# A two-block transformer kernel: latents' factors moved earlier, memory keys and values as products of rounded parts, the heads' norm taken apart, short turns placed inside projections

## The reference, cut to what matters

```python
# first block, per layer: norm, one wide projection, four mixers, output projection
h = _rmsnorm(x, norm_g[l]); p = _split(h @ w_in[l])
o_a = _mla(p["a_cq"], p["a_ckv"], ...)   # latents: _rmsnorm(cq, qa_g) @ w_uq, _rmsnorm(ckv, kva_g) @ w_ukv
o_b = _diff_attn(...); o_c = _dsa(...)   # _dsa: index scores, top-k of 128 keys for each query
o_d = _short_conv(...)
x = x + concat(o * silu(gate)) @ w_out[l]
# second block
x = x + 0.5 * swiglu(rms_norm(x, g_ffn1), ...)
proj = rms_norm(x, g_mix) @ w_in          # q, k, v of 16 heads of 64
oa = dilated_attention(first 12 heads); ob = moba_attention(last 4 heads)
ya = rms_norm(merge_heads(oa), g_out_a)   # over 768 channels
yb = rms_norm(merge_heads(ob), g_out_b)   # over 256 channels
x = x + concat(ya, yb) @ w_out
# cross attention to a memory of 256 tokens
mn = rms_norm(mem, g_mem); k, v = split(mn @ w_ckv)
x = x + attend(rms_norm(x, g_cross) @ w_cq, k, v) @ w_co
x = x + 0.5 * swiglu(rms_norm(x, g_ffn2), ...); return rms_norm(x, g_final)
```

## Time and profile before

| | |
|---|---|
| median of three runs | 1896.84 us |
| the profiled execution | 1894.07 us |
| its span, first to last instruction | 1892.3 us |
| mean granted clock of TensorE | 0.994 |
| DVE busy | 55% |
| ACT busy | 37% |
| POOL busy | 20% |
| mixing stage, steps 0 to 31 | about 1077 to 1323 us of the span |

### The profile page before, as it was taken

How to read it: one execution, slowest core, us unless ns; L and a number is a source line. 1 busy time by engine, 2 the same in 40 slices (tenths; PEclk the granted TensorE clock), 3 DMA queues, 4 the chain that set the end, 5 groups by cost and what they waited for, 6 DMA issues and landing times.

```text
span 1892.3 us, 26241 instructions
## 1 busy us (share of the span) xinstructions
PE 1850.2 (98%) x9284; PEld 1466.0 (77%) x9284; DVE 1037.5 (55%) x2106; ACT 691.6 (37%) x1274; POOL 385.6 (20%) x223
## 2 busy tenths in 40 slices
PE   7999999999999999999999999999999999999998
PEld 4767777876777788888888777777887888888887
DVE  4689787568978756554533333333544654554332
ACT  3444444444444442332232343343323432332222
POOL 2336252433534340000000222230110100000000
PEclk9999999999999999999999999999999999999999
DMA  5212212222221242323333412222221222322332
GB/s 189 68 68 79 65 48 80 91 68 68 78 67 47 78 135 94 100 92 97 100 101 110 150 46 78 78 78 79 90 89 45 68 90 98 100 94 95 103 109 89
DMA packets 48577, 165.65 MB, mean 88 GB/s; under 512 B 5592, under 2 KB 6104, under 8 KB 48472
## 3 DMA queue, kind: packets, MB, share of 16 engines
q1 hardware_dynamic: 47176, 161.88, 26.4%
q10 hardware_dynamic: 1296, 2.42, 0.4%
HBM read 162.12 MB, written 2.17 MB: 87 GB/s over the span
## 4 chain that ended last, share of the span: by engine, by line
PE 92%; DVE 3%; issue 2%; ACT 1%; POOL 1%; DMA 1%; POOLq 0%; DVEq 0%; SPq 0%; ACTq 0%
PE proj L862 73%; PE score L1078 3%; PE o L1114 2%; PE turned L1090 2%; PE proj L1233 2%; PE proj L1237 1%; PE turned L1301 1%; PE score L1295 1%; PE o L1325 1%; PE turned L832 1%; DVE wlo L1791 1%; PE o L1389 1%; PE score L1378 1%; ACT whi L1437 1%; PE proj L992 1%
## 5 line engine op out<-in xcount | busy, mean ns | idle before, releaser
L862 PE MATMUL proj<-hhi,whi 128*128 128x512 f32 x1488 | 598.9, 403 | 6.7 <-POOL wlo L655 2.6
L862 PE MATMUL proj<-hhi,wlo 128*128 128x512 f32 x1488 | 582.1, 391 | 0.0
L862 PE MATMUL proj<-hlo,whi 128*128 128x512 f32 x1488 | 581.9, 391 | 0.0
L1437 ACT ACTIVATE whi<-ring 128x1024 fp32r<-128x1024 f32 x266 | 281.4, 1058 | 679.7 <-PE proj L862 633.7
L862 PEld LDWEIGHTS proj<-hhi,whi 128*128 128x128 f32 x1488 | 280.5, 189 | 101.0 <-issue 33.9
L862 PEld LDWEIGHTS proj<-hhi,wlo 128*128 128x128 f32 x1488 | 280.5, 189 | 60.1
L862 PEld LDWEIGHTS proj<-hlo,whi 128*128 128x128 f32 x1488 | 280.9, 189 | 56.0 <-issue 1.0
L1791 DVE TENSOR_TENSOR wlo<-ring,whi 128x1024 fp32r<-128x1024 f32 x187 | 228.5, 1222 | 158.8 <-ACT whi L1437 158.7
L655 POOL TENSOR_TENSOR wlo<-ring,whi 128x1024 fp32r<-128x1024 f32 x79 | 189.8, 2404 | 445.4 <-ACT whi L1437 445.2
L668 POOL TENSOR_TENSOR prob<-prob 128x512 f32<-128x512 f32 x30 | 46.3, 1543 | 853.6 <-ACT prob L1433 853.2
L1463 ACT ACTIVATE prob<-prob,negmax 128x256 f32<-128x256 f32 (+3 forms) x208 | 114.4, 551 | 160.1 <-DVE negmax L1835 160.1
(11 more groups left out here) (219 smaller groups left out, 2211.0 us busy)
## 6 DMA issues: line engine op xcount, KB each, us to landing
ring<-wstream SPq DMA_DIRECT2D x288, 512.0 KB, 3.4
arena<-lines SPq DMA_DIRECT2D x28, 256.0 KB, 5.5
arena<-x ACTq DMA_DIRECT2D x4, 512.0 KB, 6.4
out<-arena SPq DMA_DIRECT2D x8, 256.0 KB, 2.9
arena<-mem SPq DMA_DIRECT2D x1, 1024.0 KB, 8.8
par<-params ACTq DMA_DIRECT2D x3, 74.0 KB, 1.9
arena<-hot SPq DMA_DIRECT2D x2, 85.0 KB
arena<-rope SPq DMA_DIRECT2D x1, 128.0 KB, 6.4
```

What stands on the lines that cost most here:

```text
L862: mm = pe.matmul(b, rounded(w), rounded(rhs(v, k)), start=(first and n == 0 and p == 0), stop=(last and n == len(blocks) - 1 and p == 2))
L1437: act.activation(rounded(dst), src, ACT.Copy, scale=scale).then_inc(ready, 1)
```

## The change

1. Latents. The sums of squares of CQ0, CQ1 and CKV move from chunks 1, 3, 5 of BK0 to chunks 5 and 7 of BQ0 and chunk 1 of BK0. DVE takes the means after the first half of the top-k, and makes the diagonals after the third and before it takes BK0's result; the spread stands behind the first chunk of VT0. Five top-k halves stand before the steps, the rest inside. On POOL and ACT the slot prepared after KR comes before the key's rotation.
2. Memory keys and values. KV slots are split in high and low parts like all others, the normed memory too (`memhi`, `memlo`). A key job is 8 x 3 rounded products of 128x256. Value slots are loaded so that one holds half of the contraction for two blocks of output channels; two slots make one job with a bank of 512 columns, 24 products of 128x256 each. KV12, KV13 are fills of the last window, KV14 fills steps 32 and 33.
3. Heads' norm. The pairs run in the order 6, 7, 0, ..., 5, so the group of 256 channels comes first. The six chunks of the group of 768 are scaled by gain alone and rounded as each pair ends; MIXOUT's result is multiplied by that group's factor (`residual_heads`). The two others are scaled by the ratio of the factors.
4. Turns (VN, MT), MSUM (in four parts) and MROOT are guests inside projection jobs. A guest that is a job takes the number before its host's.

```diff
+MIX_WINDOWS = (("Q1", "K1", "VT1"), ("Q2", "K2", "VT2"), ("Q3", "K3", "VT3", "KV0", "KV1"), ("Q4", "K4", "VT4", "KV2", "KV3"),
...
+    ("KV8", "KV9", "KV10", "KV11", "KV12", "KV13"))
+MIX_REST, MIX_LAST = "KV14", "KV15"
+PAIR_ORDER = (6, 7, 0, 1, 2, 3, 4, 5)
+GROUP_B = 2
+MIX_GUESTS = {"Q1": {2: "VN0", 4: "MT0"}, "K1": {4: "MT1"}, "VT1": {4: "MT2"}, "Q2": {1: "VN1", 4: "MT3"},
+              "K2": {0: "MSUM", 2: "MSUM", 4: "MSUM", 6: "MSUM"}, "Q3": {1: "VN2", 4: "MROOT"}, "Q4": {1: "VN3"},
+              "Q5": {1: "VN4"}, "Q6": {1: "VN5"}, "Q7": {1: "VN6"}, "KV8": {1: "VN7"}}
...
-LATENT_AT = ((3, 1), (3, 3), (3, 5))
+LATENT_AT = ((2, 5), (2, 7), (3, 1))
-TOPK_FIRST, TOPK_EARLY = 3, 7
+TOPK_FIRST, TOPK_EARLY = 3, 5
...
+            def load_v(n):
+                u, block = (stream_of(n) - PAIR_AT - 4 * KC) % 2, stream_of(n) // 2 * 2
+                src = bass.AP(wstream.tensor, block * P * SLOT + u * 4 * P, [[SLOT, P], [P * SLOT, 2], [1, 4 * P]])
+                sp.dma_start(ring[:, n % RING, :].rearrange("p (b n) -> p b n", b=2), src).then_inc(wload[n % RING], 16)
...
                 prepare_after("KI")
-                after_low(SLOT_OF["CQ0"])
+                prepare_after("KR")
+                after_low(SLOT_OF["CQ1"])
                 pool.wait_ge(krope_moved, L + 1)
...
-                for name in IDX_JOBS:
+                for name in IDX_JOBS[:3]:
                     prepare_after(name)
                 pool.wait_ge(mean_ready, L * 2 + 2)
                 root(2 * NT)
+                prepare_after(IDX_JOBS[3])
...
-                in_job("VT0")
-                pe.wait_ge(spread_ready, L * LAYER_ROOTS + (R_LATENT + 1))
-                spread_roots(turned[1], spread[0][:, 0:NT, :])
-                spread_roots(turned[0], spread[0][:, NT:2 * NT, :]).then_inc(spread_done, 1)
+                for k in range(KC):
+                    in_chunk("VT0", k)
+                    if k == 0:
+                        pe.wait_ge(spread_ready, L * LAYER_ROOTS + (R_LATENT + 1))
+                        spread_roots(turned[1], spread[0][:, 0:NT, :])
+                        spread_roots(turned[0], spread[0][:, NT:2 * NT, :]).then_inc(spread_done, 1)
...
+                    for p, (w, v) in enumerate(((whi[:, h, cols], memhi), (whi[:, h, cols], memlo), (wlo[:, s, cols], memhi))):
+                        mm = pe.matmul(b[:, 0:MEM], rounded(w), rounded(v[:, k, :]), start=(k == 0 and p == 0),
+                                       stop=(k == KC - 1 and p == 2))
...
+                    for p, (w, v) in enumerate(((whi[:, h, :], memhi), (wlo[:, s, :], memhi), (whi[:, h, :], memlo))):
+                        wv = w.rearrange("p (b k n) -> p b k n", b=2, k=4)[:, :, k % 4, :]
+                        mm = pe.matmul(b[:, t * MEM:(t + 1) * MEM].rearrange("p (b n) -> p b n", b=2), rounded(v[:, kk, tok]),
+                                       rounded(wv), start=(u == 0 and k == 0 and p == 0), stop=False, skip_group_check=True)
...
+            for k in range(5):
+                kv_chunk(MIX_LAST, k)
+            for n in range(GROUP_B):
+                add_squares(turned[0], NT, o2sqB[:, n, :], n == 0)
+            pe.wait_ge(o2sq_added, KC - GROUP_B - 2)
+            add_squares(turned[0], 0, o2sq[:, 0, :])
             pe.wait_ge(o2sq_ready, KC)
+            add_squares(turned[0], 0, sq[:, 0, :]).then_inc(o2sum_done, 1)
+            for k in range(5, KC):
+                kv_chunk(MIX_LAST, k)
+            made = KC - GROUP_B
+            mixout_chunks(0, range(made - 1), True)
             pe.wait_ge(spread_ready, R_HEADS + 1)
             spread_roots(turned[1], spread[0][:, 0:NT, :])
             spread_roots(turned[0], spread[0][:, NT:2 * NT, :]).then_inc(spread_done, 1)
+            mixout_chunks(1, range(made - 1))
+            mixout_chunks(0, range(made - 1, made), True)
+            mixout_chunks(1, range(made - 1, made))
+            mixout_chunks(0, range(made, KC), True)
+            mixout_chunks(1, range(made, KC))
+            for c in range(2, KC):
+                mixout_chunks(c, range(KC))
...
# ACT
+                prepare_after("KR")
                 wait_out(act, L, "KR")
                 act.activation(krope[HD:HD + 32, 1, :], krope[HD + 32:P, 1, :], ACT.Copy).then_inc(krope_moved, 1)
-                prepare_after("KR")
...
+            def heads_out(p):
+                square_heads(p)
+                if p >= GROUP_B:
+                    c = PAIR_ORDER[p]
+                    high_y2(c, gain[:, G_OUT + c:G_OUT + c + 1])
...
# DVE
-                        for n in range(TOPK_FIRST):
+                        topk_half(0)
+                        dve.wait_ge(latsum_done, L + 1)
+                        mean_squares(turned[0], ((0, 0, NT, 256), (NT, NT, NT, 128))).then_inc(mean_ready, 1)
+                        for n in range(1, TOPK_FIRST):
                             topk_half(n)
+                        spread_diag(L * LAYER_ROOTS + R_LATENT, spread[0], range(2 * NT)).then_inc(spread_ready, 1)
                     out_of(name, *early[name])
...
+            mean_squares(turned[0], ((0, 0, NT, 768), (NT, NT, NT, 256))).then_inc(heads_step, 1)
+            dve.reciprocal(ms[:, 2 * NT:3 * NT], ms[:, 0:NT]).then_inc(heads_step, 1)
+            dve.tensor_tensor(ms[:, NT:2 * NT], ms[:, NT:2 * NT], ms[:, 2 * NT:3 * NT], ALU.mult).then_inc(mean_ready, 1)
...
+            def residual_heads(c):
+                j = MIX_JOB[f"OUT{c}"]
+                dve.wait_ge(job_done, j + 1)
+                dve.tensor_tensor(tmp[:, c % 2, :], proj[j % 2][:, :], R[:, :], ALU.mult).then_inc(out_step, 1)
+                dve.wait_ge(out_step, c + 1)
+                dve.tensor_tensor(xT[:, c, :], xT[:, c, :], tmp[:, c % 2, :], ALU.add).then_inc(job_free[j % 2], 1)
```

More of the change, by code:

```diff
@@ L107 @@
 MIX_WINDOWS = (
[L108 to L119, removed]
+    ("Q1", "K1", "VT1"),
+    ("Q2", "K2", "VT2"),
+    ("Q3", "K3", "VT3", "KV0", "KV1"),
+    ("Q4", "K4", "VT4", "KV2", "KV3"),
+    ("Q5", "K5", "VT5", "KV4", "KV5"),
+    ("Q6", "K6", "VT6", "KV6"),
+    ("Q7", "K7", "VT7", "KV7"),
+    ("KV8", "KV9", "KV10", "KV11", "KV12", "KV13"))
[5 more added lines that the diff above has]
+              "Q5": {1: "VN4"}, "Q6": {1: "VN5"}, "Q7": {1: "VN6"}, "KV8": {1: "VN7"}}
+MIX_ORDER = ["Q0", "K0", "VT0"] + [part for names in MIX_WINDOWS for name in names
+                                   for part in (*dict.fromkeys(MIX_GUESTS.get(name, {}).values()), name)] \
+    + [MIX_REST, MIX_LAST] + [f"{w}{c}" for w in ("OUT", "CQ", "CO") for c in range(KC)]
+V_FIRST = [f"KV{n}" for n in range(KC, 2 * KC, 2)]
+MIX_JOBS = [name for name in MIX_ORDER if name[:2] != "VN" and name not in V_FIRST]
 MIX_JOB = {name: FFN1_JOB + FFN_JOBS + n for n, name in enumerate(MIX_JOBS)}
+for _n in range(KC, 2 * KC, 2):
+    MIX_JOB[f"KV{_n}"] = MIX_JOB[f"KV{_n + 1}"]
 MIX_TAKE = [name for name in MIX_ORDER if name[:2] not in ("VN", "MT", "MS", "MR")]
@@ L149, in is_split @@
         return n % LAYER_SLOTS not in RAW
-    return not (PAIR_AT <= n < FFN2_AT and MIX_TAKE[n - PAIR_AT][:2] == "KV")
+    return True
 def on_pool(n):
@@ L181, in half_before @@
     return SPLITS[split_no(n) - 2]
-MIX_PREP = {MIX_TAKE[half_before(n) - PAIR_AT]: n for n in range(MIX_SLOT["VT0"], FFN2_AT) if is_pair(n)}
+MIX_PREP = {MIX_TAKE[half_before(n) - PAIR_AT]: n for n in range(MIX_SLOT["VT0"], FFN2_AT) if is_pair(n) or is_kv(n)}
 FFN2_JOB = FFN1_JOB + FFN_JOBS + len(MIX_JOBS)
@@ L277 @@
 MIX_STEPS = 4 * KC
+MIX_FILLED = MIX_STEPS + 2
 def mix_plan():
-    plan = [[] for _ in range(MIX_STEPS)]
+    plan = [[] for _ in range(MIX_FILLED)]
     for w, names in enumerate(MIX_WINDOWS):
@@ L298, in mix_plan @@
             spent += cost
+    for k in range(KC):
+        plan[MIX_STEPS + k // 4].append((MIX_REST, k))
     return plan
@@ L777, in mix_low @@
                     make_low(n % RING, half_of(n), split_no(n) + 1)
-            for name in MIX_ORDER[:4]:
+            for name in MIX_ORDER[:3]:
                 mix_low(name)
[L781 to L786, removed]
+            for s in range(MIX_FILLED):
+                if s - 2 in O2_STEP and O2_STEP[s - 2] > GROUP_B:
+                    p = O2_STEP[s - 2]
+                    pool.wait_ge(o2sq_ready, p + 1)
+                    if p > GROUP_B + 1:
+                        pool.wait_ge(o2sq_added, p - GROUP_B - 1)
                     pool.tensor_tensor(o2sq[:, 0, :], o2sq[:, 0, :], o2sq[:, 1, :], ALU.add).then_inc(o2sq_added, 1)
@@ L1698, in after_mix @@
                 elif what == "KV":
-                    kv_copy(int(name[2:]))
+                    if name not in V_FIRST:
+                        kv_copy(int(name[2:]))
+                    if name in MIX_PREP:
+                        make_high2(MIX_PREP[name])
+                elif what == "MROOT":
+                    for c in range(KC):
+                        if c < KC - 1:
+                            act.wait_ge(memN_ready, c + 1)
+                        else:
```

(5 more changed lines are left out.)

198 lines of the change are left out of this document (106 added, 92 removed).

## The result

The changed kernel takes 1874.95 us (median of 4 runs, 1873.3 to 1876.5) against 1896.25 beside it (1894.1 to 1897.1): ratio 0.9889, 95% interval 0.9872 to 0.9906, so 21 us or 1.1% faster. The forecast was 1876. The profiled execution took 1873.45 us, span 1871.7, against 1894.1 and 1892.3.

A forecast was written before the change was run, and what follows sets the result against it. PE, busy 98% of the span, was taken as the bound. Terms -10.6 +1.0 +1.7 +0.3 -1.7 -0.6 -9.0 = -18.9 took 1894.1 to 1875.2, stated as 1876 us; range 1872 to 1880, with C and D 1866 to 1888.

The forecast's parts named there:

- part 1: Memory keys and values: rounded products net -10.6 us; narrow windows +1.0, KV12 and late KV14 +1.7.
- The step that was open: Price of a rounded 256-column product, nowhere in the earlier trace: taken as 0.12 us, between 0.114 and 0.228.
- five narrow windows: Places where a slot ends early in a step and the next Q waits for POOL's low part: 0.2 each, 1.0 us.
- rival C: In the KV windows preparation does not keep up, 14 slots at 0.7 more: +10, 1886 us; 15%.
- Part 2: Turns and sums inside projections: bank waits against waits removed +0.3 us, clock at the memory's squares -1.7.
- The memory's fall: Half clock of 3.4 us behind the memory's sum of squares: expected gone once split in four, -1.7 us.
- Part 3: Heads' norm: waits -1.2, clock -1.6, eight more squares +0.9, OUT2 +1.3; sum -0.6 us.
- The waits for pT: PE's waits in the last two steps, expected to go as they now lie under KV14: -1.2 us.
- Part 4: The two layers: CQ1's low part -2.6, factors -3.9, clock -1.7, first scores -0.8; sum -9.0 us.
- wait of 0.6 a layer: PE's remaining wait for the latents' diagonals at the spread, after one chunk of VT0; 1.2 us in all.
- Rival B: POOL's low catches the latents' diagonals, margin some 0.3 us: +2.4 a layer, clock falls again +1.7; 1882 us, 20%.
- weighed rule: Weight loads overlap matmuls only across row groups; part 1's products would cost 24 us more than before, not 12.6 less.

The follow-up runs named there:

- half-columns run: Changed kernel with the memory's key products over 128 of 256 tokens, the other keys left out; one run took 1873.65 us.
- f32 experiment: Changed kernel with key and value products as one f32 product of the high parts, low parts made but not multiplied; 1882.2 us, ratio 0.9936.

## Why the prediction was right, and where its terms were off

**Prices and part 1.** The step that was open, the rounded product of 256 columns, measured 0.120 as taken. The number was right, the way to it partly by luck. The row that it leaned on, an f32 instruction of 128 columns at 0.1165, had a slower first in it; from start to start that is 0.112, which is also the pace of the rounded 128-column products of the half-columns run, so it says little of what streaming costs, and the rounded form of 256 columns lies 0.008 above it, not 0.002 to 0.003. The saving was still 9.3 and not 10.6: the 256 f32 instructions took 57.6 us with their clock set right (60.6 in the trace, of which 2.9 are the half clock), not 58.7. Changes of kind cost 0.09 to 0.1 each as read from the earlier trace rows. Preparation was forecast to show at 2.7 us; it shows at 0.9, before KV12, and of the five narrow windows one opened, by 0.1. That, and the f32 experiment, in which the rate carries the gain, is what rival C fell by.

**Part 2.** Q1 0.4, K1 0.8, VT1 0.8, K2 0.3 in the waits view where I had 0.4, 0.8, 0.8, 0.1; 0.5 and not 0.3 lost against the waits of the earlier trace rows. The memory's fall went, and the block brought it back: -1.7 less the 0.5 of the changes of kind that splitting costs. The turns' new places were not tried by themselves in front of the kernel before; their 0.5 is read from the two traces.

**Part 3.** The waits for pT went (-1.2), OUT2 waits 1.6 (1.3 forecast), and the clock gave 1.7 in the profile by one fall of 3.4 us where there were 6.8. That this came out to a tenth was luck: the fall is not fixed by the code. The new order of the heads' norm was not tried by itself; its terms are read from the two traces.

**Part 4.** Forecast -9.0, measured -10.1 and -9.9 alone. The step that was off is the wait of 0.6 a layer that was to stay for the diagonals. I put PE at the spreading products one chunk after BK0, and took 0.45 for it; a chunk is three products, 0.68, and a change of kind lies behind. In the trace PE came 0.9 behind BK0's end, of which 0.07 was idle. The diagonals came at +0.8 by the mean at -4.1, close to the +0.95 forecast. Everything of the earlier trace rows there went: 3.6 + 1.5, and 2.6 before the index scores. Rival B's margin was 0.5 and not 0.3. The fall of the clock and the 0.7 of the steps went as forecast.

**Sum.** Layers -10.1, FFN +0.65, memory and mixing -11.1, start and end within 0.2: -20.6 against a forecast of -18.9. Of the -11.1 the terms above make 9.5: products 9.3, the clock at the memory 1.2 net, pT 1.2 and the clock at the heads 1.7 gained; KV12 0.9, the turns 0.5, the squares 0.9 and OUT2 1.6 lost. Waits of 0.4 us in all for a low part and a copy into the arena, in the trace of before, are not in the after one; 1.2 stays unplaced. So the sum came close with its misses partly cancelling: the products gave 1.3 less than forecast, preparation took 1.8 less, the layers gave 1.1 more, and 1.2 has no term. The forecast of 1876 also does not follow from its own working: 1875.2 for the profiled execution and 2.7 above it for the median is 1878, 3 above the measured 1874.95. And the six kinds of wait of the earlier trace rows sum to 11.5 us, not to some 8; the terms used the rows themselves, so nothing hung on it.

The weighed rule of the Trainium skill ("TensorE: Matmul & The Clock Gate", The mechanism, which is the section that states it), that only loads to other row groups overlap, would have made the 256-column product an estimated 0.216; 0.120 says no.

What stays open: why the half clock behind the heads' squares comes at all. Over the profiles with the changed kernel's form of the block it lasted 3.4 us in three, 6.8 in two and did not come in one; with the group split by three to six products it came in one of one; thinner or earlier it came in none of four. Behind the shorter block of the kernel before it lasted 6.8 us in two profiles and did not come in the third. That is a tendency for the thin forms, not a proof.

## What to carry to other kernels

Three rounded products beat one f32 product, two instructions, where each streams enough columns: with 256 it is 3 x 0.120 = 0.36 us against 2 x 0.216 = 0.43. With 128 it would be an estimated 3 x 0.112 = 0.34 against 2 x 0.112 = 0.22, a loss. So for the value jobs, which had 128 columns before, the gain rests on the new layout of their slots, which gives a product 256. It also needs engines with room to split the operands; here PE waited 0.9 us for that. Where a factor's chain crosses three engines, look at what else starts beside its last step: the diagonals clear POOL's low part by 0.5 us, and 1.7 us later they met it, for 10.8 us in the profile. A gain of one step that rests on the clock must be read from several profiles of the same code; a single one gave or took 1.7 us without any edit.

## What the runs showed that I had not expected

- A rounded 128-column product goes at 0.112 us, as an f32 instruction of 128 columns does, and one of 256 at 0.120: from 128 to 256 columns the rounded form costs next to nothing more, from 256 to 512 (0.228) nearly twice.
- Sending DVE's diagonals 1.7 us later made them 3.73 us long (1.64 alone), beside a POOL operation of 2.46 us; PE's wait became 3.9 us, and the clock fell behind it for 3.4 us in one layer and 6.8 in the other.
- The half clock has its own length: 3.4 or 6.8 us at the FFN's start with identical code in these profiles, 0, 3.4 or 6.8 behind the heads' squares. At 22 us, in the first layer, it was 6.8 in the changed kernel's profiles, and none or 10.2 in those of others with the same code there; that place costs little, since the index scores start between 61.2 and 61.8 in all of them. It goes with the spread of 2 to 3 us between runs of one kernel: the changed kernel's first four took 1873.3 and 1873.5 at a mean granted clock of 0.995, and 1876.4 and 1876.5 at 0.992 and 0.993.
